# Placing the expert search of tiles 2 and 3 behind the first U rows, in a new order over heads

## The reference

```python
q = (xb @ wq).reshape(TOKEN_BLOCK, PEER_HEADS, 2, PEER_DQ // 2)     # 8 heads
s = jnp.einsum('thcd,ckd->thck', q, subkeys)                        # 2 x 128 scores a head
sv, si = lax.top_k(s, PEER_TOPK)                                    # 16 best of each
cand = (sv[:, :, 0, :, None] + sv[:, :, 1, None, :]).reshape(...)
top_v, top_pos = lax.top_k(cand, PEER_TOPK)                         # 16 best of 256 sums
eidx = jnp.take_along_axis(cidx, top_pos, axis=-1)                  # 128 experts a token
u = u_tab[eidx]
a = jax.nn.gelu(jnp.einsum('td,thkd->thk', xb, u), approximate=False)
v = v_tab[eidx]
return jnp.einsum('thk,thkd->td', g * a, v)
```

## Time and profile before

| | us |
|---|---|
| Median of 3 runs | 4904.73 |
| The profiled execution | 4913.59 |
| Its span in the trace | 4911.6 |
| First U row of tile 0 is issued | 1189.0 |
| First V product of tile 0 on PE | 1804.0 |
| Last `mix_out` of the mixer in `merged` | 2979.7 |

### The profile page before, as it was taken

The page is one execution under the profiler, slowest core; times in us unless marked ns, Lnnn a source line. Parts: engine busy times, 40 slices in busy tenths (PEclk is TensorE's granted clock), DMA queues, the critical chain, the costliest instruction groups (busy, mean ns, idle before and its releaser), DMA issues.

```text
span 4911.6 us, 37680 instructions
## 1 busy us (share of the span) xinstructions
PE 3594.1 (73%) x11523; PEld 1496.1 (30%) x11523; DVE 2939.1 (60%) x7683; ACT 439.7 (9%) x1069; POOL 2275.6 (46%) x2122
## 2 busy tenths in 40 slices
PE   5698989885554288888887884677666677666677
PEld 3354535353333233333333331322122122111111
DVE  4455556564787746576676673857656657666600
ACT  2111212120000011011111110000000000000000
POOL 0000000001222227576575663567767767777764
PEclk7799989897777699899898996899899999988899
DMA  4214223223444569999899987799999999999998
GB/s 149 56 40 122 76 88 112 77 87 125 137 141 133 158 231 368 334 346 381 303 369 351 321 320 286 260 374 392 367 364 372 377 375 384 370 373 379 367 315 289
DMA packets 454272, 1285.69 MB, mean 262 GB/s; under 512 B 77136, under 2 KB 160648, under 8 KB 452040
## 3 DMA queue, kind: packets, MB, share of 16 engines
q0 software_dynamic: 308768, 1129.45, 62.6%
q1 hardware_dynamic: 145320, 154.07, 9.6%
HBM read 1244.15 MB, written 39.20 MB: 261 GB/s over the span
## 4 chain that ended last, share of the span: by engine, by line
PE 21%; DMA 19%; POOL 15%; DVE 13%; issue 7%; SPq 1%; ACT 0%; DVEq 0%; POOLq 0%; ACTq 0%
DMA c_vb<-in_peer_v,c_idxT 13%; POOL c_vb L1909 8%; PE c_acc L2089 7%; PE c_pj L2027 7%; POOL c_ub L1909 7%; DVE c_ub L2453 3%; DMA c_ub<-in_peer_u,c_idx 3%; PE c_pj L1951 2%; PE c_pW L1976 2%; DMA out_p_n<-c_extra 1%; DMA c_extra<-tail_d 1%; DVE c_extra L2302 1%; DVE c_extra L2298 1%; DVE c_es L2304 1%; DVE c_si L2265 1%
## 5 line engine op out<-in xcount | busy, mean ns | idle before, releaser
L2089 PE MATMUL c_acc<-c_vb,c_Z 128*32 128x512 f32 x4096 | 1433.4, 677 | 590.8 <-DMA c_vb<-in_peer_v,c_idxT 589.4
L2453 DVE CUSTOM_DVE_ANT_0 c_ub<-c_ub,c_h 128x1024 f32<-128x1024 f32 x1024 | 1242.1, 1224 | 844.8 <-DMA c_ub<-in_peer_u,c_idx 839.0
L1909 POOL DMA_INDIRECT c_ub<-in_peer_u,c_idx x1024 | 1078.8, 1054 | 917.1 <-DVE c_a L2453 584.2
L1909 POOL DMA_INDIRECT c_vb<-in_peer_v,c_idxT x1024 | 1139.5, 1113 | 612.5 <-PE c_acc L2089 381.8
L2089 PEld LDWEIGHTS c_acc<-c_vb,c_Z 128*32 128x32 f32 x4096 | 258.2, 116 | 1592.6 <-DMA c_vb<-in_peer_v,c_idxT 1096.8
L2027 PE MATMUL c_pj<-weights,c_extra 128*128 128x512 f32 (+1 forms) x1280 | 522.7, 560 | 47.2 <-DMA weights<-in_w_in 47.2
L826 PE MATMUL b_pj<-weights,b_hcB 128*128 128x512 f32 (+1 forms) x1280 | 525.0, 568 | 1.1 <-ACT b_s_v L1054 1.1
L482 POOL DMA_DIRECT2D weights<-in_w_in x40 | 36.1, 910 | 661.8 <-PE b_pj L826 647.6
L2027 PEld LDWEIGHTS c_pj<-weights,c_extra 128*128 128x128 f32 x1280 | 241.8, 194 | 325.2 <-issue 317.8
L826 PEld LDWEIGHTS b_pj<-weights,b_hcB 128*128 128x128 f32 x1280 | 247.6, 195 | 253.2 <-issue 246.1
L1976 PE MATMUL c_pW<-weights,c_extra 128*128 128x256 f32 (+1 forms) x720 | 209.2, 447 | 6.8 <-ACT c_extra L2117 6.8
(11 more groups left out here) (438 smaller groups left out, 3401.9 us busy)
## 6 DMA issues: line engine op xcount, KB each, us to landing
weights<-in_w_in POOLq DMA_DIRECT2D x32, 1024.0 KB, 8.0
weights<-in_w_in SPq DMA_DIRECT2D x32, 1024.0 KB, 34.6
c_ub<-in_peer_u,c_idx POOLq DMA_INDIRECT x1024, 6.3
c_vb<-in_peer_v,c_idxT POOLq DMA_INDIRECT x1024, 6.3
b_hcB<-hT_d SPq DMA_DIRECT2D x16, 512.0 KB, 5.4
b_s_C<-in_state_mlstm_c SPq DMA_DIRECT2D x8, 1024.0 KB, 12.4
out_s_c<-b_s_C SPq DMA_DIRECT2D x8, 1024.0 KB
c_extra<-hT_d SPq DMA_DIRECT2D x16, 512.0 KB, 7.2
```

Source lines behind the costliest of these rows:

```text
L1909: nc.gpsimd.indirect_dma_start(out=out, out_offset=None, in_=io[table], in_offset=bass.IndirectOffsetOnAxis(ap=at, axis=0)).then_inc(loade ...
L2089: last = nc.tensor.matmul(acc[half][j * SUB:(j + 1) * SUB, :], Z[:, lo:lo + SUB], vb[:, turn % RV, half * 512:(half + 1) * 512], start=Fal ...
L2453: nc.vector.tensor_tensor_reduce(ub[:, turn % RU, :], ub[:, turn % RU, :], h2[:, b, :], 1.0, 0.0, ALU.mult, ALU.add, a[:, b, k:k + 1]).the ...
```

## The change

Two things change, both only in the order of the list; no instruction is added or taken away.

First, the order inside a search. Before, head hd's scores stand one `q` behind its own `q`, and `best`, `sums`, `pick` directly behind the scores. Now it is a pipeline over heads: at step t the list has `q` of head t, `best` of head t - 3, `qT` of head t - 1, `sums` of head t - 3, `sc` of head t - 2 and `pick` of head t - 3. In the three steps behind the last `q`, the first items of the next tile's search may be put in (`ending`).

Second, the spread. Period -1 gets the search of tile 1 alone. Tiles 2 and 3, the mixer and tile 4's search go over 376 slots of periods 0 to 2. Items are no longer counted but weighed with a table of estimated durations.

```diff
+COST = {"out": 3.6, "norm2": 4.5, "hT": 2.4, "q": 3.6, "qT": 0.8, "sc": 0.8, "best": 2.4, "sums": 2.2, "pick": 2.6,
...
+def search_items(n, after_head, ending):
+
+    order = [("hT", n, 0)]
+    for t in range(PH + 3):
+        if t < PH:
+            order += [("q", n, t)]
+        else:
+            third = len(ending) * (t - PH) // 3
+            order += ending[third:len(ending) * (t - PH + 1) // 3]
+        if t >= 3:
+            order += [("best", n, t - 3)]
+        if 1 <= t < PH + 1:
+            order += [("qT", n, t - 1)]
+        if t >= 3:
+            order += [("sums", n, t - 3)]
+        if 2 <= t < PH + 2:
+            order += [("sc", n, t - 2)]
+        if t >= 3:
+            order += [("pick", n, t - 3)] + after_head(t - 3)
...
-    for n in range(1, C0):
-        first += prepare_items(n)
-    first += mixer_items() + prepare_items(C0)
...
-    until = C0 * SLOTS - 8
...
-            share = len(first) * (s + 1) // until
-            order += first[at:share]
...
+    spans = [(with_rows_in(chain(range(1, SOON + 1)), 1), 0, SLOTS - 8),
+             (chain(range(SOON + 1, C0)) + mixer_items() + with_rows_in(prepare_items(C0), C0), SLOTS, C0 * SLOTS - 8)]
+    for n in range(C0 + 1, TILES):
+        items = prepare_items(n)
+        lo = (n - 1) * SLOTS
+        spans.append((with_rows_in(items, n) if n < CHUNKS else items, lo, lo + SLOTS - 10))
+    work = [[] for _ in slots]
+    for items, lo, hi in spans:
+        cost = [COST.get(what, 0.0) for what, n, k in items]
+        done_cost, total = 0.0, sum(cost)
+        for item, c in zip(items, cost):
+            work[lo + min(int((hi - lo) * done_cost / total), hi - lo - 1)].append(item)
+            done_cost += c
```

More of the change, by code:

```diff
@@ L1354, in place, with begin_items @@
     return m // C1, C0 + m % C1, m % 2
[L1357 to L1370, removed]
+COST = {"out": 3.6, "norm2": 4.5, "hT": 2.4, "q": 3.6, "qT": 0.8, "sc": 0.8, "best": 2.4, "sums": 2.2, "pick": 2.6,
+        "softmax": 1.0, "idxT": 0.5, "p": 3.6, "gate": 2.0, "pre": 2.5, "t1": 1.5, "powers": 1.2, "conv": 1.0,
+        "kq": 1.8, "tap": 1.2, "ev": 0.7, "y": 1.2, "ey": 0.7, "qk": 3.0, "s2": 3.0, "s2e": 1.2, "att": 1.5, "s3": 3.2,
+        "num": 1.3, "squares2": 1.0, "cst": 1.3, "mix": 4.5, "s4": 0.8, "mT": 0.5}
+def begin_items(n):
+    order = [("search_in", n, 0)] if n in (0, C0) else []
+    return order + [("tile_in", n, 0)] + [("out", n, k) for k in range(4)] + [("norm2", n, 0), ("x2_out", n, 0)]
+def search_items(n, after_head, ending):
[16 more added lines that the diff above has]
+            order += [("pick", n, t - 3)] + after_head(t - 3)
+    order += [("softmax", n, 0)]
     if n < CHUNKS:
@@ L1373, in prepare_items @@
     return order
+def prepare_items(n, ending=()):
+    return begin_items(n) + search_items(n, lambda hd: [], list(ending))
 def mixer_items():
@@ L1461, in rows_items @@
     return slots
+SOON = 1
 EARLY = 3 * (PH - 1)
 def merged_schedule():
[L1469 to L1475, removed]
-    slots = rows_items()
-    first, other = [], []
-    for n in range(1, C0):
-        first += prepare_items(n)
-    first += mixer_items() + prepare_items(C0)
@@ L1481, in merged_schedule, with early_rows @@
-    first.insert(first.index(("x2_out", 1, 0)) + 1, ("h2_in", 1, 0))
-    first.insert(first.index(("x2_out", C0, 0)) + 1, ("h2_in", C0, 0))
-    until = C0 * SLOTS - 8
[L1484 to L1487, removed]
-            share = len(first) * (s + 1) // until
-            order += first[at:share]
[L1490 to L1500, removed]
+    def early_rows(hd):
+        return [("u", 0, 3 * hd + t) for t in range(3)] if hd < PH - 1 else []
@@ new lines, in with_rows_in, with chain @@
+    def with_rows_in(items, n):
+        at = items.index(("x2_out", n, 0)) + 1
+        return items[:at] + [("h2_in", n, 0)] + items[at:]
+    order = with_rows_in(begin_items(0), 0) + search_items(0, early_rows, [])
+    slots = rows_items()
+    def chain(tiles):
+        items = begin_items(tiles[0]) if tiles else []
+        for n in tiles:
+            items += search_items(n, lambda hd: [], begin_items(n + 1) if n + 1 in tiles else [])
+        return items
+    spans = [(with_rows_in(chain(range(1, SOON + 1)), 1), 0, SLOTS - 8),
+             (chain(range(SOON + 1, C0)) + mixer_items() + with_rows_in(prepare_items(C0), C0), SLOTS, C0 * SLOTS - 8)]
@@ L1501, in merged_schedule @@
+    for background, slot in zip(work, slots):
+        order += background + slot
     return order
```

## The result

The changed kernel takes 4870.61 us (median of 5 runs, 4868.46 to 4878.99); the kernel before, in the same comparison, 4897.98 us. The ratio is 0.9935, 95% interval [0.9919, 0.9951]: faster by 0.65%. The prediction had said 4822 us, 1.7% faster. The direction was right, the size was not: some 50 us of the expected gain didn't come. Times and ratios here are medians of several executions; the lengths of stretches are read from the one traced execution of each kernel. Executions of one kernel spread by 7 to 40 us, so a difference of some 15 us in one stretch of one trace is weak evidence by itself.

What follows compares the result with a forecast made beforehand. DVE was taken to bound period -1, DMA the periods from 3191 us on. 1500 + 240 + 44 + 1130 + 190 = 3104 where 3191 was, -87; with -5 later, 4913.6 - 92 = 4822 us, range 4770 to 4875.

Steps and rivals of the forecast that it cites:

- The head order in tile 0: Search of tile 0: first scores stand behind a third q, about +5 us, bounds 0 and +8.
- Period -1: Tile 0's U rows with one tile's search: first V product at 1500 us, about -299, from 1481 to 1532.
- Tiles 2 and 3: Their search in period 0 beside V rows 0 to 56: 240 us, DVE 90% busy, bounds 216 and 300.
- The stall for the mixer's weights: Moves from the border into period 0, PE stopping at the first projection: 44 us, bounds 35 and 55.
- The mixer: V rows 56 to 347: 1130 us, PE and DMA both at 88%, 70.6 us a step, bounds 1030 and 1250.
- the slower rival: Mixer: its chain through PE, DVE and ACT keeps 78.1 us a step, 1250 us; 4942 in all; chance 0.15.
- DMA alone: Rival: DMA alone sets the mixer's time, 1030 us, 4722 in all; chance 0.16.
- the sign that the chain and not the work sets the step: Mixer: PE's clock below 0.9, or PE's longest waits on DVE and not on V rows.
- Tile 4: Load stall stays, 54.15 us; search falls from 154 to 135 us; together 190, bounds 165 and 209.
- Periods 3 to 6: DMA at 0.99 stays the limit, an even spread finds little: -5 us, bounds -15 and +10.
- The rule of the Trainium skill: Mixer: weight loading share, 32 to 34%, measures PE's limit; so PE has room and DMA alone sets the time.
- The third rival: Period -1: U rows take 2.5 to 3 us each, 270 to 320 us; 4865 to 4920 in all; chance 0.11.

Runs made afterwards that it cites:

- five buffers: The changed kernel with five U buffers instead of four, nothing else: 0.9887 of the kernel before.
- place alone: The kernel before with only tiles 2 and 3 moved behind tile 0's first rows, old order over heads, items counted: 0.9928 of the kernel before.
- the experiment with the taps: Changed kernel with tile loads weighed and tile 1's search begun early, plus the mixer's 18 small convolution-tap loads moved behind its weights: 0.9866 of the kernel before.
- the missing lead alone: Changed kernel with items counted, but a tile's loads weighing nothing: 0.9958 of the kernel before; periods 3 to 6 took 1458 us.
- the fastest version: Changed kernel with tile loads weighed, tile 1's search begun beside tile 0's last heads, and five U buffers: 4790.38 us, 0.9763 of the kernel before.

## Why the prediction was wrong

*What bounds the kernel* held: DVE in period -1, DMA from 3191 on. *The head order in tile 0* was +5 us and measured +5 (first U row at 1194.3 for 1189.0); the exact hit is luck, since in the other runs with the new order that row came at 1194 to 1201.

*Period -1* is the step that failed: 1500 us forecast for the first V product, 1546 measured, beyond the step's own upper bound of 1532. Two terms of its sum carry the miss. The search's tail of tile 0 still stands there, 21 us of DVE in which three rows pass; it was there before as well (20 us), and the sum left it out. The stretch without scores took 77 us, not 50: its 37 rows took 2.1 us each and not 1.5. One cause shown is the ring's round trip, 6.0 us in the median and not 4.4, and five buffers gave back 15 us of the whole period, 6 of them here. The sum also lacks POOL's time: it was busy 46 us here with issuing 36 rows, 1.3 us each, and with the 0.3 between two issues that is 1.6 us a row without any wait. The two other terms were near: the rows with search took 149 us and the search behind the last row 19, together 168 where 172 were given; and 15 us of products passed before the first V product, where 13 were allowed for them, gelu and weights. The order shown ahead of the prediction had tile 2's products between the residual and the first V product, and they were not priced. Together 21 + 27 - 4 + 2 = 46 us.

*Tiles 2 and 3*: 240 forecast, 250 measured. The reason given for it was wrong: the old order over heads took 242 us for some 48 rows of each kind (place alone) with DVE busy 82%, the same share as in the new order with 56 rows, and not the 90% expected. In the new order DVE waited for scores only twice in this stretch, 24.0 us, and in the old order twice, 22.7 us; so there was nothing between the heads to remove.

*The stall for the mixer's weights*: 44 forecast, 34 measured; and the experiment with the taps shows that shortening it further does not bring the first mixer step forward by itself.

*The mixer*, the boldest term: 1130 forecast, 1106 measured, with PE busy 87% (960 of 1106) and DMA at 0.90. `mix_out` came every (2935.5 - 1931.5) / 15 = 66.9 us on average, where 78.1 was the pace before. So the slower rival, which kept the pace of 78.1, is refuted, and so is DMA alone, which would have given 1030.

```profile
L1887 SPq DMA_DIRECT2D mixT_d<-c_extra x16: 337/344/6095, 1931.5 to 2935.5; - x16
```

But that 88% came out for both engines is partly luck, for the reason given doesn't hold on PE's side: rows of V hardly hold PE back any more. Of PE's 146 idle us in this stretch, 10.9 were waits for V rows, where it had waited 89.0 in two of the three stretches before. The other waits are on DVE and ACT, 134 us, 28 of them at the borders of periods. These are the largest and the one for V rows:

```profile
PE c_pW L2097 <- DVE c_extra L2439: 42.3, 14, 6.0
PE c_acc L2111 <- DMA c_vb<-in_peer_v,c_idxT: 10.9, 9, 2.4
```

The prediction had named this as the sign that the chain and not the work sets the step. It came true, though PE's clock stayed at 0.93: PE's own queue, its work and its waits for the chain, now sets the step. Whether DVE was late for its chain's sake, or because U rows stand in its queue too (it waited 194.5 us for them), was not tested.

*Tile 4*: 190 forecast, 47 + 163 = 210 measured, just beyond the bound of 209. The search was to fall from 154 us to 135 by the pipeline and took 163. Its three pieces show why: from the first product to `x2_out`, the heads, and the border. Before:

```profile
3037.00:3061.00 24.00, 19.34 (x48) 7.03 (x48) 6.00 (x17) 0.00 (x0) 5.04 (x5) 0.93 0.33 110
3061.00:3174.00 113.00, 80.31 (x321) 44.73 (x325) 98.15 (x340) 8.81 (x20) 57.69 (x55) 0.83 0.79 265
3174.00:3194.00 20.00, 12.90 (x37) 2.65 (x29) 7.76 (x15) 1.30 (x4) 13.31 (x13) 0.67 0.77 256
```

After:

```profile
2983.00:3011.00 28.00, 22.88 (x56) 8.06 (x56) 5.99 (x17) 0.00 (x0) 8.78 (x9) 0.87 0.50 165
3011.00:3126.00 115.00, 73.35 (x301) 43.74 (x305) 94.05 (x331) 7.94 (x20) 48.11 (x47) 0.77 0.67 228
3126.00:3146.00 20.00, 14.01 (x40) 2.80 (x32) 7.60 (x16) 2.12 (x5) 11.60 (x11) 0.66 0.69 237
```

Before, most of DVE's idle time lay at the two ends, 18 of 24 us and 12 of 20, where there is nothing to search yet or nothing more; among the heads it was busy 98 of 113 us already. A share over 154 us had been read as if it were even.

*Periods 3 to 6* are the second step that failed: -5 forecast, +17 measured, beyond the bound of +10. "An even spread finds little" took the weights for an even spread. They are even for the engines' work, but not for a load and the product that waits for it. With items counted these periods took 1443 us, 21 less than before; the weights took 38 back, 25 of them in the rows behind the weightless load and 16 by the missing lead alone.

The steps together: 46 + 10 - 10 - 24 + 20 = 42 us to the end of period 2, +22 in periods 3 to 6, -4 behind them: 60. The profiled execution misses the sum by 57 (4879 us against 4822); the other 3 come from the start of period 3, which the sum had at 3191 before, while the event used here stood at 3194.

The rule of the Trainium skill that was weighed ("Perfetto Trace Analysis", "Identifying the Most-Contended Engine") would have made the mixer 1030 us. PE's share of weight loading there rose to 36% (403.6 of 1106), which by the rule is room; yet the stretch took 1106 us, with DMA at 0.90 and PE's idle time nearly all waits for DVE and ACT.

The third rival, that period -1 doesn't shrink as it says, was nearest to what happened there: 230 us for the 107 rows, 2.15 a row where it had 2.5 to 3. Its reason, a longer round trip, is a part of it: the fifth buffer gave back 15 of the 46 us.

## What to carry to other kernels

When a list of weights spreads work over a pipeline, give every item that starts a transfer a weight too: here the lead between a load and its first use was worth more than the evenness of the rest, since the wait holds back everything behind it in the queue. Before expecting a better order to fill an engine's idle share, cut the stretch at its start, middle and end and see where the idle time lies. A round trip read from the first transfer, with none ahead of it, is a lower bound and not the pace of a busy ring, and the time to issue a transfer belongs in the sum beside it.

## What the runs showed of the hardware

A DMA share of 0.98 was not yet the floor: periods 3 to 6 of 1464 us at 0.98 and 375 GB/s in the kernel before took 1420 us in the fastest version, at 381 to 390 GB/s. A fifth buffer for the U rows went with a part of this in the kernel before (1464 to 1444 us, nothing else edited), but not in the change (1481 and 1485 us), so that it is the buffer's doing is not shown. What the share of 0.98 leaves out was not looked into.
